# Half A's last feed-forward part in seven block products, with half B's residual in DRAM meanwhile

## The reference, cut to what matters

```python
def swiglu_ffn(h, w_gate, w_up, w_down):
    return (jax.nn.silu(h @ w_gate) * (h @ w_up)) @ w_down
...
        xp = xp + mp
        xs = xs + ms
        xp = xp + swiglu_ffn(rms_norm(xp, g_ffn[i]), w_gate[i], w_up[i], w_down[i])
        xs = xs + swiglu_ffn(rms_norm(xs, g_ffn[i]), w_gate[i], w_up[i], w_down[i])
```

## Time and profile before

| | us |
|---|---|
| median of 3 runs (2161.72 to 2163.22) | 2162.99 |
| the profiled execution's own time | 2162.42 |
| its span, first to last instruction | 2160.6 |
| TensorE busy | 2136.2 |
| VectorE busy | 1423.6 |
| GpSimd busy | 1340.6 |
| ScalarE busy | 1165.5 |

### The profile page before, as it was taken

The page is one execution under the profiler, slowest core; times in us unless marked ns, Lnnn a source line. Parts: engine busy times, 40 slices in busy tenths (PEclk is TensorE's granted clock), DMA queues, the critical chain, the costliest instruction groups (busy, mean ns, idle before and its releaser), DMA issues.

```text
span 2160.6 us, 35879 instructions
## 1 busy us (share of the span) xinstructions
PE 2136.2 (99%) x13360; PEld 1934.6 (90%) x13360; DVE 1423.6 (66%) x2345; ACT 1165.5 (54%) x2023; POOL 1340.6 (62%) x812
## 2 busy tenths in 40 slices
PE   9899999999999999999999999999999999999999
PEld 8798877888889789999999898888888889999998
DVE  5998788863434578888886455455555257665665
ACT  7556664533424666777763466565656334444443
POOL 3787889976446557675766644343433455868775
PEclk9999999999999999999999999999999999999999
DMA  5112323332333523222234342222222223233232
GB/s 158 49 50 59 88 83 98 98 98 88 98 98 99 140 75 98 76 83 83 76 98 133 97 98 85 88 82 84 79 87 80 85 85 114 89 118 112 80 103 81
DMA packets 314938, 198.43 MB, mean 92 GB/s; under 512 B 41398, under 2 KB 287758, under 8 KB 314510
## 3 DMA queue, kind: packets, MB, share of 16 engines
q1 hardware_dynamic: 312888, 195.03, 30.7%
q10 hardware_dynamic: 1878, 1.11, 0.2%
HBM read 186.49 MB, written 7.19 MB: 90 GB/s over the span
## 4 chain that ended last, share of the span: by engine, by line
PE 85%; DVE 9%; POOL 2%; issue 2%; ACT 1%; DMA 0%; SPq 0%; DVEq 0%; POOLq 0%; ACTq 0%
PE ps L613 37%; PE ps L1051 10%; PE ps L969 9%; PE ps L873 7%; DVE ps L2331 4%; PE ps L1080 4%; PE ps L1007 4%; PE ps L880 4%; PE ps L1088 2%; PE ps L1015 2%; PE ps L844 1%; PE ps L829 1%; PE ps L647 1%; DVE hBl L2228 1%; PE ps L805 1%
## 5 line engine op out<-in xcount | busy, mean ns | idle before, releaser
L3078 POOL TENSOR_TENSOR wlo<-raw,whi 128x1024 fp32r<-128x1024 f32 x218 | 542.1, 2488 | 541.9 <-PE ps L613 325.7
L613 PE MATMUL ps<-hAh,whi 128*128 128x512 f32 x1056 | 410.1, 392 | 2.3 <-ACT hAh L1489 0.9
L613 PE MATMUL ps<-hAl,whi 128*128 128x512 f32 x1056 | 408.0, 390 | 0.2
L1438 ACT ACTIVATE whi<-raw 128x1024 fp32r<-128x1024 f32 x218 | 230.4, 1057 | 312.0 <-PE ps L613 176.3
L613 PE MATMUL ps<-hAh,wlo 128*128 128x512 f32 x1056 | 267.8, 396 | 0.0
L3213 POOL TENSOR_TENSOR wlo<-raw,whi 128x512 fp32r<-128x512 f32 x124 | 174.4, 1417 | 113.4 <-ACT whi L1944 103.6
L613 PEld LDWEIGHTS ps<-hAh,whi 128*128 128x128 f32 x1056 | 198.0, 188 | 46.0 <-ACT hAh L1478 1.7
L613 PEld LDWEIGHTS ps<-hAl,whi 128*128 128x128 f32 x1056 | 198.3, 188 | 41.7 <-DVE hAl L2228 1.2
L613 PEld LDWEIGHTS ps<-hAh,wlo 128*128 128x128 f32 x1056 | 194.9, 188 | 42.4 <-issue 4.1
L3109 POOL TENSOR_TENSOR accp<-accp,prod 128x574 f32<-128x574 f32 (+1 forms) x136 | 192.3, 1414 | 29.6 <-ACT prod L1572 18.3
L2426 DVE TENSOR_TENSOR xB<-ps,xB 128x544 f32<-128x544 f32 x184 | 132.4, 720 | 99.0 <-PE ps L613 42.4
(11 more groups left out here) (429 smaller groups left out, 5465.8 us busy)
## 6 DMA issues: line engine op xcount, KB each, us to landing
raw<-in_w_gate_dram SPq DMA_DIRECT2D x58, 512.0 KB, 3.8
raw<-in_w_up_dram SPq DMA_DIRECT2D x58, 512.0 KB, 3.8
raw<-in_w_down_dram SPq DMA_DIRECT2D x54, 512.0 KB, 3.5
raw<-in_w_pw_dram SPq DMA_DIRECT2D x38, 512.0 KB, 3.8
raw<-in_w_down_dram SPq DMA_DIRECT2D x44, 256.0 KB, 3.2
raw<-in_w_gate_dram SPq DMA_DIRECT2D x40, 256.0 KB, 2.9
raw<-in_w_up_dram SPq DMA_DIRECT2D x40, 256.0 KB, 2.9
raw<-in_w_qkv_dram SPq DMA_DIRECT2D x32, 256.0 KB, 3.6
```

The source lines that it names most:

```text
L613: ins = nc.tensor.matmul(o, wt[n % 2][:, P * k:P * (k + 1)], src[h][:, k, c0:c0 + w], start=start, stop=stop)
L1438: nc.scalar.activation(whi[n % 2][:], raw[n % 2][:], ACT.Copy).then_inc(w_hi, 1)
L3078: nc.gpsimd.tensor_tensor(wlo[n % 2][:], raw[n % 2][:], f(whi[n % 2][:]), ALU.subtract).then_inc(w_lo, 1)
```

## The change

Half A's stage in layer 1 becomes a seven-product stage as well. `ffn_v` takes an object `S` that says which half it serves. For half A:

- the products have 256 columns, in the order A11, A22, A12, S3, S2, S4, S1 (a, f, c, d, b, g, e), and use banks 0 to 3 and 7 without changing places from pair to pair;
- S2, S3 and S4 are written over A11, A21 and A12 in `raw`, and S1 into the free half of `sq`; so SP can load the next A11 only when S2's low part is made and S4 is summed;
- the activations' sums lie where `x["B"]` was, which SP writes to DRAM in `qkv("B")` and reads back in two parts around `wo("B")`; the scores of the sample frames use bank 4 alone, with a wait in between;
- the low part of the activated pairs 1 to 9 (`acl`) is made by GpSimd, two instructions in each G, behind the low parts of weight blocks 4 and 6 of the pair; for the pairs 0 and 10 VectorE still makes it;
- `ffn_va` is VectorE's order for it. In `qkv("B")` VectorE makes x_norm, three sums and the low parts in the order that it had for the other half.

```diff
+            u1h = sb("u1h", [P, 4, 256], F32R, c)
...
+        x = {"A": xa, "B": sb("xB", [P, KD, N["B"]])}
...
+                else:
+                    self.win = self.win0 = ["A11", "A22", "A12", "S3", "S2", "S4", "S1"]
+                    self.sums0 = ["S1", "S3", "S2", "S4"]
+                    self.blocks = 18 * (NG - 2) + 14
...
+            if S.h == "A":
+                return {"a": 0, "c": 0, "d": 1, "f": 2, "b": 3, "e": 3}[z]
...
                 for G in range(1, NG):
+                    v_products(S, "G", G)
+                    v_products(S, "U", G)
+                    nxt[0] = v_bank(S, G, "d") if S.h == "B" else 0
+                    if S.h == "B" or G < NG - 1:
+                        v_down(S, G - 1)
...
+                wo("B")
+                down(1, "A", NG - 2, lambda: norm_mean("ffn1B"), 0)
+                down(1, "A", NG - 1, None, 2)
```

SP's room for a load of half A's stage, and the end of the stage on SP:

```diff
+                        name = {"A11": "S2", "A12": "S4"}.get(name, name)
+                        sp.wait_ge(S.lo, v_low_of(S, j, name))
+                        sp.wait_ge(S.sum, v_sums(S, j, {"S2": "S4", "A22": "S1"}.get(name, name)))
...
+                for d in range(2):
+                    wo_tile(d)
+                freed(sp, ("V", "A", "U", NG - 1, "b"))
+                sp.dma_start(x["B"][:, 4:8, :], x_spill["B"][:, 4:8, :]).then_inc(S.x_back[1], 16)
+                full(sp, ("V", "A", "U", NG - 1, "e"))
+                sp.dma_start(x["B"][:, 0:4, :], x_spill["B"][:, 0:4, :]).then_inc(S.x_back[0], 16)
```

ScalarE's order within a G of either stage (the same list as before the change, with `S`), cut to the steps that the prediction names:

```diff
+                    v_high(S, m + 4)
                     turned_high(att, prev, 0)
...
                     out_part(att, prev, 0)
+                    v_high(S, m + 7)
                     turned_high(att, prev, 1)
+                    v_silu(S, G, "c")
                     out_high(att, prev, 0)
+                    v_high(S, m + 8)
+                    v_high(S, m + 9)
+                    v_silu(S, G, "d")
                     out_part(att, prev, 1)
+                    v_silu(S, G, "e")
+                    v_copied(S, "U", G)
```

VectorE's new order, its first part:

```diff
+            def ffn_va(S):
...
+                    if G > 1:
+                        v_weight_sum(S, j, "S2")
+                    linked()
+                    read_scores(att, cur, 0)
+                    turned_low(att, prev, 0)
+                    v_weight_sum(S, j, "S4")
+                    v_sum_up(S, "G", G, "d")
+                    v_sum_up(S, "G", G, "f")
+                    out_sum(att, prev, 0)
+                    v_sum_up(S, "G", G, "b")
+                    turned_low(att, prev, 1)
...
+                    v_weight_sum(S, j + 1, "S1")
+                    read_scores(att, cur, 1)
+                    if G > 1:
+                        v_sum_up(S, "G", G, "e")
+                        v_last_sums(S, "G", G)
+                    v_weight_sum(S, j + 1, "S3")
+                    v_weight_sum(S, j + 1, "S2")
```

And GpSimd's:

```diff
+                    if S.h == "A" and m > 18 and m % 18 in (4, 6):
+                        e, cols = m % 18 // 2 - 2, dest(S.h)
+                        pool.wait_ge(act_hi, S.base + 2 * (m // 18) + e + 1)
+                        nc.gpsimd.tensor_tensor(acl[e][:, cols], s_[e][:, cols], f(ach[e][:, cols]), ALU.subtract
+                                                ).then_inc(act_lo, 1)
```

1056 lines of the change are left out of this document (561 added, 495 removed).

## The result

The changed kernel takes 2174.14 us (median; 2173.92 to 2174.46), the one before, on the same chip, 2162.97: a ratio of 1.0053, with a 95% interval of 1.0036 to 1.007. It is slower, by 11.2 us, where 11.7 us less were forecast; 2174.14 lies above the range of 2145 to 2162.

What follows compares the result with a forecast made beforehand. TensorE's instructions were taken to bound the kernel. From the profiled 2162.4 us, - 18.0 + 1.0 + 2.7 + 2.0 + 0.6 = - 11.7 gave 2150.7, and 0.6 up to the median 2151.3 us, range 2145 to 2162.

Steps and rivals of the forecast that it cites:

- TensorE's own work: Half A's stage: 168 matmuls of 256 columns at 0.120 us replace 96 of 512; 1.80 us less per G, 18.0 in ten.
- The steady pairs: Product part of each steady G: three tight places, taken as a 0.3 us stall in each of nine G, 2.7 us.
- The two moved instructions: Activations' low parts, moved from VectorE to GpSimd: claimed to relieve VectorE fully and load GpSimd fully; 1.5 us each.
- rival 3: Low parts before `down`: GpSimd becomes the bound and the kernel slower, 2169.3 us at 1.75 us per instruction; chance 0.12.
- Rival 2: U's product f: weight loads land at 3.5 to 4 us, not 2.9, so each U waits; 2157.6 us; chance 0.15.
- The start of the stage: Half A's first products: idle TensorE, judged from half B's 2.65 us; bounds 0 and 2.7, taken as 1.0 us.
- The first tile of w_o: End of half A's stage: its load waits for S4's low part, so TensorE waits about 2.0 us; bounds 0 and 4.
- Hidden work: Half B's residual (back in 9.5 us, wanted after 12.1) and activation sums in `qkv("B")`: no stall, nothing counted.
- Rival 1: Half A's stage: no stall in the three tight places and an early w_o tile; 2146 us; chance 0.08.
- rival 4: Half A's products: 256-column matmuls cost what 272 columns do, 0.126 us each; 2161.3 us; chance 0.05.
- The sample scores: Sample frames' scores in one bank instead of two: two waits of about 0.3 us, 0.6 us in all.
- the second place: Bank 1 for the second `down` tile, wanted 1.88 us after product e: 0.6 us to spare claimed.

Runs made afterwards that it cites:

- e14: Changed kernel with all of GpSimd's weight-block low parts in half A's stage cut from 512 to 16 columns; 2150.49 us, ratio 0.9945.
- e1: Changed kernel with two of VectorE's small sink copies in each G moved behind the sums that follow them; 2167.37 us, ratio 1.0027.
- e5: Changed kernel with the four sink copies of each G in half A's stage on ScalarE instead of VectorE; 2167.67 us, ratio 1.0024.
- e6: Changed kernel with sink copies on ScalarE, activations' low parts on VectorE again and unit 2's ptl earlier; 2163.57 us, ratio 1.0005.
- e2: Changed kernel with the activations' two low parts of each G back on VectorE, none on GpSimd; 2169.02 us, ratio 1.0034.
- e8: Changed kernel with GpSimd's low parts of the activations cut from 512 to 8 columns; 2168.76 us, ratio 1.0029.
- e13: Changed kernel with GpSimd's low parts of the stage's first 8 weight blocks cut from 512 to 16 columns; 2169.76 us, ratio 1.0035.
- e4: Changed kernel with ScalarE's first two weight copies of half A's stage ahead of the fourth activation term's copy; 2174.12 us, ratio 1.0057.
- e9: e6 plus two pieces of the first w_o tile issued before S4's low part is done; 2161.88 us, ratio 0.9997.
- the repairs: On e6: w_o pieces issued earlier, query 3's high parts earlier, then sum e and SiLU's second copy earlier; with all, 2160.50 us, ratio 0.9993.

## Why the prediction was wrong, point by point

- **TensorE's own work, -18.0 us.** Right: 0.119 us for a 256-column matmul, 36.7 to 36.8 us for a G without a wait. e14, whose stage is nearly free of waits, shows it: 36.7 us in four of its G.
- **The steady pairs, 0.3 us of stall in a G.** This is the step that failed: 2.7 us in the sum for nine G, where TensorE stood for some 2.4 us in each, 19 us in eight. The place was right (U's f, spare time 0.1 us), the load was on time (2.96 us), and the order of the chain was right. Wrong was the list "ptl (0.69), S1 (1.14), two scores (0.96) and the sum of e (0.44)" and the "two scores, ptl and S4" ahead of it: `read_scores` ends with a copy of the sinks, which I left out as too small to count. Two of these stand in the chain, for 2.1 us, and S1 took 1.56 there. Together 2.5 us, against 2.3 us by which silu of d was late. e1 and e5 show that the two copies made that place bind, and e14 that the meetings with GpSimd did. The copies are not shown to be all of the 2.4 us, since a second wait, for ptl of unit 2, lay just under the first (e1, e6). Of the signs that the prediction named, an idle TensorE ahead of U's f came, but behind late sums and not a late load; GpSimd's mean (1.3 us) and VectorE's idle time in the product part (22.7 us busy of 28.0) showed nothing.
- **Durations from other stretches.** The means for ptl and for the two scores, from half A's stage, held: both read PSUM. The ones that do not carry over are those of instructions in SBUF. S1 had 1.14 us and has 1.29 on average here, and the copy, 380 ns in half A's stage, where GpSimd works for 14.8 of 38.6 us, goes to 904 ns with 26.2 of 39.2. The sentence "the two engines hold each other up" was in the prediction, with 1.52 against 0.68 us as its rows, but it was used only to ask if GpSimd would be late. It had to be put into each such VectorE instruction in the tight chain.
- **The two moved instructions, counted as relief of VectorE.** Wrong in sign. Off GpSimd, in whatever way, they give 4 to 5 us back (e2, e8). The Trainium skill has the rule that decides it (SBUF — State Buffer, section "SBUF: two separate sides"): whichever of a VectorE instruction of certain kinds and a GpSimd instruction comes first has the shared ports to its end, and the other one waits. The trace agrees: the copy of 1459.09 ends with GpSimd's low part. By that rule 0.68 us of VectorE were exchanged for 1.3 us in which VectorE may have to wait. The prediction cited it and drew rival 3 from it, a late GpSimd, when what it makes late here is VectorE.
- **Rival 3, GpSimd as the bound, 2169.3.** It had the right sign and nearly the right time by luck, for another reason. GpSimd's mean was 1.34 us, below the 1.45 of the sum and the 1.75 that this rival needs, and no wait of TensorE in the steady G was for it.
- **Rival 2, late loads, 2157.6.** The place was its place; the loads were not late (`w_up`'s land after 3.0 us in the median from 1376 to 1690 us, 2.9 forecast).
- **The start of the stage, +1.0.** 5.0 us by the milestones, which also hold the 1.8 us that the first G's products save, so 6.8 in the terms of the sum. The comparison with half B's start counted products and not how long VectorE takes in the first 10 us. e13 shows that 4.8 of it (3.9 by the ratios) hang on GpSimd's first eight low parts, by meetings for the most part; in e4 another order on ScalarE did not help. The other 2 us are open.
- **The first tile of w_o, +2.0.** 2.95 us; the mis-sized term is the issue of a piece, for which the sum had 0.25 us, a value that no row of the kernel before shows, and which took 0.66. e9 shows it: two issues less in front, 1.4 us less wait. The 1.6 us of half clock behind the wait were in no term, and the kernel before had them in another place.
- **Hidden work.** Right: nothing in the waits points at half B's residual (back in 6.7 us) or at the sums in `qkv("B")`.
- **Rival 1 and rival 4.** Neither: the distance between two starts was the forecast's, not 0.126 us, and there were stalls.
- **The sample scores, +0.6.** Some 1.2 us. Before, the two heads' matmuls of a unit start in pairs 0.01 us apart, and the six take 0.50 us; now they come one after the other and take 1.11, in two units (from 1653.57 and 1660.29 us). The loss is less the wait than the missing overlap.
- **A slip in the second place.** 1.88 less 0.44 and 0.7 leaves 0.7 us and not 0.6. Nothing hangs on it.

Open is how far a version without cuts can get. e6 with the repairs has a G of 37.8 us against 37.03 in e14, and a start that is still some 4.5 us late.

## What to carry to other kernels

Before a chain with tenths of a us to spare is trusted, list every instruction that the engine issues in it, copies of a few numbers too, and add the wait for a GpSimd instruction (here 1.3 us) to each that works on SBUF alone, as an upper bound of its price. Moving an instruction from VectorE to GpSimd took 0.68 us off VectorE here and put 1.3 us of GpSimd in its way; I would expect it to pay only where VectorE's SBUF work is not on the path. When one wait is taken away the next may lie 1 us beneath it, so gains of single edits are not added up: here it took three to free the G.
